# Two layers of attention on one core: the probabilities turned as two halves of 64 query rows in the scores' tiling, the reciprocals spread by products beside the results

## What is computed

```python
def even_mixer(...):                      # layer 1
    ya, ya_c = global_gqa(qa, ka, va, qa_c, ka_c, va_c, ctx_out)
    yb, yb_c = neighbourhood_attention(qb, kb, vb, qb_c, kb_c, vb_c, rpb, ctx_out)
def odd_mixer(...):                       # layer 2
    y, yc = window_gqa_sink(q, k, v, qc, kc, vc, sink, ctx_out)

# each of them, for a block of 128 queries and one head of 64 features:
    p = jax.nn.softmax(gqa_scores(q, k), axis=-1)   # queries x keys (with a bias, a window or a sink)
    y = gqa_out(p, v)                               # queries x 64
```

## Time and profile before

| | |
|---|---|
| median of 3 runs | 2410.93 us (2410.2 to 2414.32) |
| span of the profiled execution | 2412.5 us, 33093 instructions; no other time was taken of it |
| attention of layer 1 | 978.1 to about 1144 us |
| attention of layer 2 | 1858.8 to 1985.6 us |
| granted clock of TensorE in their middle | 1.00 of 2.4 GHz |

### The profile page before, as it was taken

How to read it: one execution, slowest core, us unless ns; L and a number is a source line. 1 busy time by engine, 2 the same in 40 slices (tenths; PEclk the granted TensorE clock), 3 DMA queues, 4 the chain that set the end, 5 groups by cost and what they waited for, 6 DMA issues and landing times.

```text
span 2412.5 us, 33093 instructions
## 1 busy us (share of the span) xinstructions
PE 2322.8 (96%) x13146; PEld 1885.5 (78%) x13146; DVE 1549.3 (64%) x2465; ACT 949.7 (39%) x1768; POOL 350.6 (15%) x455
## 2 busy tenths in 40 slices
PE   6999899999999899999999999999999999999998
PEld 3876567888887788777888888888887778888886
DVE  3648686576767652566779985656474767765457
ACT  4426464322222521576352242332452774423333
POOL 0110100001022210101100313223112120101131
PEclk9999999999999899999999999999999999999999
DMA  6330024744534312110412433324122103432321
GB/s 265 124 106 22 26 87 159 262 161 157 169 136 166 105 53 81 69 62 2 174 66 88 135 127 122 98 95 140 45 79 79 37 13 146 152 110 88 105 88 70
DMA packets 79177, 257.56 MB, mean 107 GB/s; under 512 B 5680, under 2 KB 10416, under 8 KB 70576
## 3 DMA queue, kind: packets, MB, share of 16 engines
q1 hardware_dynamic: 65024, 205.01, 24.6%
q0 software_dynamic: 12704, 46.14, 5.5%
q10 hardware_dynamic: 1296, 4.30, 0.5%
HBM read 246.00 MB, written 9.44 MB: 106 GB/s over the span
## 4 chain that ended last, share of the span: by engine, by line
PE 86%; DVE 7%; ACT 3%; issue 2%; DMA 1%; SPq 1%; POOL 1%; POOLq 0%; DVEq 0%; ACTq 0%
PE PS L1300 11%; PE PS L1301 11%; PE PS L1302 11%; PE PS L1371 6%; PE PS L1373 6%; PE PS L1372 6%; PE PS L1177 4%; PE PS L1196 3%; PE PS L1216 3%; PE PS L1008 3%; PE PS L1011 3%; PE PS L1009 3%; PE PS L1269 2%; PE PS L1272 2%; PE PS L1270 2%
## 5 line engine op out<-in xcount | busy, mean ns | idle before, releaser
L1300 PE MATMUL PS<-HH,WH 128*128 128x512 f32 (+1 forms) x1088 | 420.3, 386 | 3.1 <-DVE WL L2387 1.7
L1301 PE MATMUL PS<-HL,WH 128*128 128x512 f32 (+1 forms) x1088 | 416.7, 383 | 0.0
L1302 PE MATMUL PS<-HH,WL 128*128 128x512 f32 (+1 forms) x1088 | 416.7, 383 | 0.0
L2797 ACT ACTIVATE WH<-STG 128x1024 fp32r<-128x1024 f32 (+1 forms) x202 | 196.9, 1023 | 269.0 <-PE PS L1373 225.4
L2387 DVE TENSOR_TENSOR WL<-STG,WH 128x1024 fp32r<-128x1024 f32 (+1 forms) x202 | 241.2, 1235 | 36.8 <-ACT WH L2797 36.6
L1300 PEld LDWEIGHTS PS<-HH,WH 128*128 128x128 f32 x1088 | 204.4, 188 | 47.8 <-issue 6.4
L1920 DVE SCALAR_TENSOR_TENSOR ACC<-ADAW,CS,ACC 128x1024 f32<-128x1024 f32 x168 | 227.1, 1387 | 21.7 <-PE PS L1011 14.4
L1302 PEld LDWEIGHTS PS<-HH,WL 128*128 128x128 f32 x1088 | 204.4, 188 | 40.4
L1301 PEld LDWEIGHTS PS<-HL,WH 128*128 128x128 f32 x1088 | 204.5, 188 | 39.8 <-issue 1.0
L1371 PE MATMUL PS<-WH,AH 128*128 128x512 f32 x600 | 234.9, 392 | 0.3 <-DVE AL L2615 0.3
L1372 PE MATMUL PS<-WL,AH 128*128 128x512 f32 x600 | 233.6, 389 | 0.0
(11 more groups left out here) (273 smaller groups left out, 4452.6 us busy)
## 6 DMA issues: line engine op xcount, KB each, us to landing
STG<-in_w_up SPq DMA_DIRECT2D x66, 1024.0 KB, 6.0
ADAW<-in_w_ada SPq DMA_DIRECT2D x96, 512.0 KB, 3.8
STG<-in_w_down SPq DMA_DIRECT2D x20, 1024.0 KB, 5.2
ADAW<-in_w_ada POOLq DMA_DIRECT2D x32, 512.0 KB, 4.1
STG<-in_w_ffn_out SPq DMA_DIRECT2D x10, 1024.0 KB, 6.2
STG<-in_ev_w_in SPq DMA_DIRECT2D x8, 1024.0 KB, 5.1
STG<-in_w_in SPq DMA_DIRECT2D x6, 1024.0 KB, 6.9
spill<-X POOLq DMA_DIRECT2D x10, 512.0 KB, 5.1
```

The costliest lines, as they stand in the source:

```text
L1300: e.matmul(out, h_, hh, start=c == 0, stop=False)
L1301: e.matmul(out, h_, hl, start=False, stop=False)
L1302: return e.matmul(out, l_, hh, start=False, stop=c == 7)
L2797: return e.activation(dst, src, ACT.Copy)
```

## The change

`turn` now makes two transposes of each chunk: the query rows 0 to 63 go through the array's upper 64 rows to bank 5, the query rows 64 to 127 through the lower 64 rows to bank 6, each 64 columns wide. Both heads' first four chunks are one unit, the rest of both a second one. ScalarE copies bank 5's half of every unit, VectorE bank 6's. `inverse` spreads the reciprocals by plain products with the identity, one for each half of 64 columns. The order of a step becomes: scores of i, second unit of i-2 (where there is one), reciprocals of i-2, result of i-2, first unit of i-1. VectorE copies the second unit of i-2 between the two maxima of i; ScalarE copies it first in its step and the first unit of i-1 between the two heads' exponentials.

```diff
         def turn(p, u):
-            it, b = items[p], 5 + turns[0] % 2
-            turns[0] += 1
-            k.bank["T", L, p, u] = b
-            free(b)
-            unit = turned_units(it)[u]
+            unit = turned_units(items[p])[u]
+            for r in range(2):
+                free(5 + r)
             for i, (j, o) in enumerate(unit):
                 w.wait_ge(*k.ac_exp((L, p, j)))
-                m = e.transpose(PS[:, b, i * P:(i + 1) * P], k.p_place(L, p, j)[:, o:o + P], ident)
+                for r in range(2):
+                    q = slice(64 * r, 64 * r + 64)
+                    m = e.transpose(PS[:, 5 + r, 64 * i:64 * i + 64], k.p_place(L, p, j)[q, o:o + P], ident[q, q])
             m.then_inc(*k.pe_pt.up((L, p, u)))
-            freed[b] = [(k.dv_ptc if copied_by_dve(it, u) else k.ac_ptc)((L, p, u))]
+            freed[5], freed[6] = [k.ac_ptc((L, p, u))], [k.dv_ptc((L, p, u))]
...
             for t in range(items[p]["nq"]):
-                m = e.transpose(PS[:, 7, 256 + t * P:384 + t * P], k.spread(p)[:, t * P:(t + 1) * P], ident)
+                for j in range(2):
+                    m = e.matmul(PS[64 * j:64 * j + 64, 7, 256 + t * P:384 + t * P],
+                                 k.spread(p)[:, t * P + 64 * j:t * P + 64 * j + 64], ident, start=True, stop=True)
...
-            for u in range(len(turned_units(it))):
-                w.wait_ge(*(k.dv_ptc if copied_by_dve(it, u) else k.ac_ptc)((L, p, u)))
             n, nq = it["nk"] // P // it["nq"], it["nq"] * P
             for c in range(n):
+                w.wait_ge(*k.ac_ptc((L, p, c // 4)))
+                w.wait_ge(*k.dv_ptc((L, p, c // 4)))
...
             if i >= 2:
+                if len(turned_units(items[i - 2])) > 1:
+                    turn(i - 2, 1)
                 inverse(i - 2)
+                result(i - 2)
             if 1 <= i <= N:
                 turn(i - 1, 0)
-            if i >= 2:
-                result(i - 2)
-            if 1 <= i <= N:
-                for u in turning_order(items[i - 1])[1:]:
-                    turn(i - 1, u)
...
+def half_turned(k, L, p, it, u, r):
+
+    n = len(turned_units(it)[u]) // 2
     o = 3072 + p % 2 * 1536
+    to = k.att[L]["HT"][:, o:o + 1536].rearrange("p (j c q) -> p j c q", j=2, q=P)[:, :, 4 * u:4 * u + n, 64 * r:64 * r + 64]
+    return to, k.PS[:, 5 + r, 0:128 * n].rearrange("p (j c q) -> p j c q", j=2, q=64)
...
         for i in range(N + 2):
             if i < N:
                 largest_of(i, 0)
+            if i >= 2:
+                turned_p(i - 2, 1)
+            if i < N:
                 largest_of(i, 1)
...
             if 1 <= i <= N:
-                copies(i - 1)
+                turned_p(i - 1, 0)
...
         for i in range(N + 2):
-            if 1 <= i <= N:
-                turned_p(i - 1, 0)
             if i >= 2:
+                turned_p(i - 2, 1)
                 inverse(i - 2)
             if i < N:
                 powers(i, 0)
             if 1 <= i <= N:
-                turned_p(i - 1, 1)
+                turned_p(i - 1, 0)
```

More of the change, by code:

```diff
@@ L1161, in woven_pairs @@
     def woven_pairs(L, items):
-        N, turns = len(items), [0]
+        N = len(items)
         def free(b):
@@ L1762, in turned_units, with last_turned @@
     if it["nq"] == 2:
[L1763 to L1787, removed]
-    o = 3072 + p % 2 * 1536
[L1789 to L1796, removed]
+        return [[(j, 256 * t + c * P) for j in range(2) for c in range(2) for t in range(2)]]
+    return [[(j, c * P) for j in range(2) for c in cs] for cs in (range(min(4, n)), range(4, n)) if len(cs)]
+def last_turned(it):
+    return len(turned_units(it)) - 1
+def half_turned(k, L, p, it, u, r):
+    n = len(turned_units(it)[u]) // 2
+    o = 3072 + p % 2 * 1536
+    to = k.att[L]["HT"][:, o:o + 1536].rearrange("p (j c q) -> p j c q", j=2, q=P)[:, :, 4 * u:4 * u + n, 64 * r:64 * r + 64]
+    return to, k.PS[:, 5 + r, 0:128 * n].rearrange("p (j c q) -> p j c q", j=2, q=64)
 def layer0_items(k):
@@ L2282, in result, with turned_p @@
                             ALU.mult).then_inc(*k.dv_out.up((L, p)))
-        def copies(p):
+        def turned_p(p, u):
             it = items[p]
[L2286 to L2291, removed]
+            if u > last_turned(it):
+                return
+            w.wait_ge(*k.pe_pt((L, p, u)))
+            if p >= 2:
+                w.wait_ge(*k.pe_out((L, p - 2)))
+            e.tensor_copy(*half_turned(k, L, p, it, u, 1)).then_inc(*k.dv_ptc.up((L, p, u)))
         for i in range(N + 2):
@@ L3019, in turned_p @@
             it = items[p]
-            if u >= len(turned_units(it)) or copied_by_dve(it, u):
+            if u > last_turned(it):
                 return
@@ L3024, in turned_p @@
                 w.wait_ge(*k.pe_out((L, p - 2)))
-            copy(unit_place(k, L, p, it, u), unit_bank(k, L, p, it, u)).then_inc(*k.ac_ptc.up((L, p, u)))
+            copy(*half_turned(k, L, p, it, u, 0)).then_inc(*k.ac_ptc.up((L, p, u)))
         def inverse(p):
@@ L3040, in powers @@
             if p >= 2:
-                w.wait_ge(*k.pe_pt((L, p - 2, last_turned(items[p - 2], j))))
+                w.wait_ge(*k.pe_pt((L, p - 2, last_turned(items[p - 2]))))
             for t in range(nq):
```

## The result

The changed kernel takes 2385.07 us (median; 2384.24 to 2388.7) beside 2412.62 for the kernel before: a ratio of 0.9884, with an interval of 0.987 to 0.9899. It is 1.2% or some 28 us faster; 2376 was forecast, with 2362 to 2398 as the range.

A forecast was written before the change was run, and what follows sets the result against it. TensorE, busy 40 of 40 us in both attention stretches, was taken as the bound. 21.6 - 8.6 + 30.6 = 43.6 us gross, less 7.5 of stalls and 1.2 at stage ends, gave 34.9 off 2410.93: 2376 us, range 2362 to 2398.

The forecast's parts named there:

- Changes of tiling: TensorE's attention steps: two changes of array tiling instead of four, gaining 0.30 us an item, 21.6 us over 72 items.
- Reciprocals: On TensorE, two plain products replace a transpose per 128 queries; 80 blocks at 0.1075 us cost 8.6 us.
- Twins: Pairs of 64-row half transposes replacing a chunk's full one: 0.062 us against 0.1075, gaining 30.6 us over 672 chunks.
- A: Rival: weight load sets the half transposes' pace, 0.1075 us a pair; only tiling changes gain, 2398 us; chance 0.14.
- C: Rival: the two row halves don't overlap in transpose mode, 0.215 us a chunk; slower, 2470 us; chance 0.07.
- D: Rival: transposes still change the array's mode and a pair costs a full transpose; no change, 2410 us; chance 0.04.
- Copies: Copies of transposed halves out of PSUM raise VectorE to 83% and ScalarE to 80% busy, under the bound.
- B: Rival: copies, writing runs of 64 elements, become the bound at 0.2 us more each; 2390 us; chance 0.12.
- sign for B: TensorE's short waits for VectorE's or ScalarE's copy adding up to over 10 us would show slower copies bind.
- Waits: TensorE's stalls in the attention steps, 7.5 us together, plus 1.2 us of copies at the stages' ends.
- Step (c): Four wide steps of each layer where ScalarE and VectorE split a quarter of output weights: 0.4 us each, 3.2 in all.
- Step (a): VectorE's copy of a wide unit's second half-block between two maxima comes late; TensorE waits about 0.05 us.

The follow-up runs named there:

- e2: Changed kernel with full 128x128 transposes in the new order, head 0 to bank 5, head 1 to bank 6, whole blocks copied: 2416.06 us, ratio 1.001.
- e3: Changed kernel with the reciprocals transposed as before, one 128x128 transpose per 128 queries: 2389.22 us, ratio 0.9896.
- e1: Changed kernel with a unit's half transposes issued all of rows 0 to 63 first, then all of rows 64 to 127: 2402.64 us, ratio 0.9951.
- e8: Changed kernel with VectorE's quarter of the output weights one step later, ahead of the smaller item's maxima: 2383.73 us, ratio 0.9876.
- e5: Changed kernel with the output weights split in eight half-size pieces over eight steps of each layer, not four: 2390.36 us, ratio 0.9903.
- e12: e5 with layer 1's bias tables of heads 4 and 5 fetched ahead of the output weights' second half: 2380.43 us, ratio 0.9864.
- e4: Changed kernel with ScalarE copying both halves of the second unit, VectorE none between its maxima: 2379.35 us, ratio 0.9852.
- e10: Changed kernel's half transposes and products for the reciprocals, but in the order of the kernel before on all three engines: 2413.73 us, ratio 1.0003.

## Why the forecast was right, and where it was off

- **What bounds it**: right. TensorE set the pace before and does after, but for the pairs with a quarter, where the chain leaves it. The granted clock stayed at 1.00.
- **Changes of tiling, 0.30 us an item**: right. The scores' pieces fell by 0.14, the change between results and transposes stayed; e2 puts the changes back and the pieces grow by the same sizes.
- **Reciprocals, 8.6 us**: right in size (0.37 with the change, as 0.15 + 0.22); e3 shows that the part pays for itself and no more.
- **Twins at 0.062 us**: measured 0.0625. The row of the two-row transposes was the right one to go by, and A, C and D fall with it. It was a better ground than I saw: line 1448 works on rows 0 and 1 and on rows 64 and 65, so that row did show two row groups transposing at once, which the prediction, under C, says no row does (e1 has the starts). By the rule of the Trainium skill in TensorE: Matmul & The Clock Gate, LDWEIGHTS, a twin would have stayed at 107 ns; the measurement decides against it here, at a granted clock of 1.00. From 30.55 to 30.95 us, where the granted clock was 0.50, that is at the 1.2 GHz level, the loads of line 1448 on one row group do start 0.107 us apart (30.631, 30.737 and 30.844).
- **Copies**: VectorE was put at 83% and came to 80% in layer 1 and 84% in layer 2; ScalarE at 80%, and came to 72% and 74%. B's mechanism didn't come: a copy of 512 in runs of 64 takes 689 ns on VectorE against 684. The prediction's sign for B, waits of over 10 us, did come (15.7 were lost), so that sign couldn't tell slower copies from waits by place; the copies' own length could.
- **Waits**: this is the term that failed, in size. Step (c), a quarter of the weights, was put at 0.4 us each, 3.2 in all, and cost 7.7. I set the 1.2 us against the slack of a whole step; but the work stood at one place of the queue, ahead of the maxima on which ScalarE and then TensorE depend, with little slack behind it: by the chain above the next first maximum starts only when VectorE's quarter ends, and TensorE's fifth chunk stands still for 0.48 us. e8 shows that the place is worth 0.7 of the 1.03 us, e5 and e12 that the size of the pieces is. Step (a) was 0.05 for a wide item and is about 0.22 (e4). The timeline of the changed kernel shows where, in the lines below: the first maximum starts 0.21 us after the first half transpose, where the layout had 0.1, and by the single records the next product starts 0.15 us after the copy's end (1068.32 to 1068.47), for which it had nothing. VectorE wasn't late by its own queue: it had stood idle for 0.58 us until the scores were there. Together 8.7 us were forecast, ends included, and 15.7 lost. That is the 7 us between 34.9 and the 27.9 of the stages. (Two small slips in the prediction change nothing: 0.075 x 16 is 1.2 and not 1.3, and the pair of about 6.1 us is 6.21 by its own sum; 6.34 was measured.)

```profile
1067.03 0.96 DVE L2246 TENSOR_REDUCE SM<-PS 128x1 f32<-128x768 f32 x1 [0.58 <-PE PS L1177]
...
1067.91 0.41 DVE L2271 COPY HT<-PS 128x256 f32<-128x256 f32 x1
...
1068.44 0.23 PEld L1218 LDWEIGHTS PS<-HT,REG 128*64 128x64 f32 x4 [0.21 <-issue]
```

- **What no rival held**: that halves and order help only together, with the units of both heads as they are here (e10, e2). The forecast priced them as terms of one sum, which is right for the whole change and would have been wrong for either part.

## What to carry to other kernels

When the bound engine gets 15% faster, the others' waits must be costed by their place in the queue, not by the slack of a step: lay out the dependent chain behind each long extra instruction, and cut or move it. Two edits that are each worth nothing can be worth much together, when one takes away TensorE's work and the other takes away the wait that this work was hiding. And look at what stands behind a wait in a DMA queue before moving the work that ends it.

## What the runs showed of the hardware that I had not expected

- A float32 transpose of 64 rows streams beside one on the other 64 rows, each half to a bank of its own, at 0.0625 us a pair, where a full one of the same chunk takes 0.1075 to 0.109.
- TensorE starts work on one row half ahead of earlier instructions for the other half (e1): in a queue of eight and eight the second half starts 0.31 us after the first and not 0.5, and a score's load goes ahead of the last transposes' loads. The loads of line 1448 do the same in the trace of before: the fifth starts second.
- The change of tiling, with the first load behind it, is 0.15 us into the full array or 128x64 and 0.14 into 64x128 for transposes; into 64x128 for scores, with their longer load, 0.20.
